# Column groups for a decay tree and for one layer's attention values, and four edits to VectorE's order, in a two-model transformer kernel

## The reference

```python
x = first_block(x, ...)          # layer 0 "even": gated convolution and pooling; layer 1 "odd"
return second_block(x, ...)      # layers 2 and 3, "hyb": hybrid_mixer

def odd_mixer(...):              # 8 heads: softmax(q k' + decay bias) v, and a 31-tap convolution
def hybrid_mixer(h, ...):
    a_out = rmsnorm(dilated_attention(rope(aq), rope(ak), av))
    o = gla_chunked(gq, gk, gv, log_sigmoid(z) / 16)    # gated linear attention, 4 heads
    g_out = rmsnorm(o) * silu(gr)
    return concatenate([a_out, g_out]) @ w_out

def gla_chunked(q, k, v, g):     # what it computes, without the chunks
    b = cumsum(g)
    attn[t, s] = sum_d q[t, d] k[s, d] exp(b[t, d] - b[s, d])    for s <= t
    return attn @ v
```

## Time and profile before

| | us |
|---|---|
| median of 3 runs | 1201.57 (1200.78 to 1203.65) |
| the profiled execution | 1202.72 |
| its span, first to last instruction | 1200.9 |
| PE busy | 1180.9 (98%) |
| PEld busy | 969.2 (81%) |
| DVE busy | 757.3 (63%) |
| ACT busy | 601.1 (50%) |
| granted clock of PE, mean | 0.999 |

### The profile page before, as it was taken

The page is one execution under the profiler, slowest core; times in us unless marked ns, Lnnn a source line. Parts: engine busy times, 40 slices in busy tenths (PEclk is TensorE's granted clock), DMA queues, the critical chain, the costliest instruction groups (busy, mean ns, idle before and its releaser), DMA issues.

```text
span 1200.9 us, 16977 instructions
## 1 busy us (share of the span) xinstructions
PE 1180.9 (98%) x5878; PEld 969.2 (81%) x5878; DVE 757.3 (63%) x1055; ACT 601.1 (50%) x896; POOL 44.5 (4%) x78
## 2 busy tenths in 40 slices
PE   8999999999999999999999999999999999999997
PEld 6877888888868888888778888888888878888886
DVE  4788545548887765554777676456366777755541
ACT  4555534425865554352555665445356566644530
POOL 0200000000001000000100100000010011000000
PEclk9999999999999999999999999999999999999999
DMA  7667765735633775662565157666626524856540
GB/s 255 186 226 223 250 205 179 232 116 164 206 122 107 226 243 179 209 220 96 164 203 177 50 166 257 195 195 208 192 84 223 167 72 133 266 180 209 165 150 35
DMA packets 161086, 214.14 MB, mean 178 GB/s; under 512 B 13137, under 2 KB 104953, under 8 KB 161024
## 3 DMA queue, kind: packets, MB, share of 16 engines
q1 hardware_dynamic: 155840, 201.52, 52.6%
q10 hardware_dynamic: 4896, 11.58, 2.9%
q0 software_dynamic: 288, 0.23, 0.2%
HBM read 212.22 MB, written 1.06 MB: 178 GB/s over the span
## 4 chain that ended last, share of the span: by engine, by line
PE 50%; DVE 0%; issue 0%; ACT 0%; POOL 0%; POOLq 0%; DVEq 0%; ACTq 0%
PE ps L577 15%; PE ps L579 15%; PE ps L578 15%; PE ps L920 2%; PE ps L1084 1%; PE ps L978 0%; PE ps L734 0%; PE ps L726 0%; PE ps L950 0%; PE ps L741 0%; PE ps L970 0%; PE ps L967 0%; PE ps L997 0%; PE ps L996 0%; PE ps L995 0%
## 5 line engine op out<-in xcount | busy, mean ns | idle before, releaser
L1540 DVE TENSOR_TENSOR w_lo<-raw,w_hi 128x1024 fp32r<-128x1024 f32 x377 | 446.9, 1222 | 132.6 <-ACT w_hi L1150 129.3
L1150 ACT ACTIVATE w_hi<-raw 128x1024 fp32r<-128x1024 f32 x377 | 381.2, 1054 | 137.4 <-PE ps L579 70.5
L577 PE MATMUL ps<-w_hi,a_hi 128*128 128x512 f32 x1040 | 414.2, 398 | 4.6 <-DVE w_lo L1540 1.6
L579 PE MATMUL ps<-w_hi,a_lo 128*128 128x512 f32 x1040 | 406.2, 391 | 0.0
L578 PE MATMUL ps<-w_lo,a_hi 128*128 128x512 f32 x1040 | 405.3, 390 | 0.0
L577 PEld LDWEIGHTS ps<-w_hi,a_hi 128*128 128x128 f32 x1040 | 195.6, 188 | 47.7 <-DVE a_lo L1558 3.4
L579 PEld LDWEIGHTS ps<-w_hi,a_lo 128*128 128x128 f32 x1040 | 195.5, 188 | 41.9
L578 PEld LDWEIGHTS ps<-w_lo,a_hi 128*128 128x128 f32 x1040 | 195.8, 188 | 37.9
L577 PE MATMUL ps<-w_hi,h_hi 128*128 128x512 f32 x480 | 188.6, 393 | 0.5 <-DVE h_lo L2002 0.4
L579 PE MATMUL ps<-w_hi,h_lo 128*128 128x512 f32 x480 | 187.0, 390 | 0.0
L578 PE MATMUL ps<-w_lo,h_hi 128*128 128x512 f32 x480 | 186.8, 389 | 0.0
(11 more groups left out here) (220 smaller groups left out, 763.6 us busy)
## 6 DMA issues: line engine op xcount, KB each, us to landing
raw<-ffn_w_in SPq DMA_DIRECT2D x176, 256.0 KB, 4.2
raw<-w_in SPq DMA_DIRECT2D x96, 256.0 KB, 3.2
raw<-ffn_w_out SPq DMA_DIRECT2D x88, 256.0 KB, 3.9
raw<-w_gate SPq DMA_DIRECT2D x88, 256.0 KB, 3.7
raw<-w_up SPq DMA_DIRECT2D x88, 256.0 KB, 4.4
raw<-w_down SPq DMA_DIRECT2D x88, 256.0 KB, 4.2
raw<-od_w_in SPq DMA_DIRECT2D x40, 256.0 KB, 3.0
raw<-ev_w_in SPq DMA_DIRECT2D x32, 256.0 KB, 4.3
```

The lines of the kernel that those rows point to most:

```text
L577: nc.tensor.matmul(ps[:, bank, :], hi, wh, start=first, stop=False)
L579: return nc.tensor.matmul(ps[:, bank, :], lo, wh, start=False, stop=last)
L1150: nc.scalar.activation(w_hi[:, v.slot, :], raw[:, v.raw, :], ACT.Copy).then_inc(w_high, 1)
L1540: V.tensor_tensor(w_lo[:, v.slot, :], raw[:, v.raw, :], w_hi[:, v.slot, :].bitcast(F32), ALU.subtract).then_inc(w_low, 1)
```

## The change

- `first_chunks`: at the first feed-forward boundary (kk = 1) PE turns tile 1 ahead of the third unit of the second chunk, not of the fourth.
- `after_boundary` and `boundary` on DVE: for k = 0 one unit fewer is fed ahead of tile 1's boundary; for k = 3 (the one boundary with a layer norm and a norm of the next model in one) a unit that was fed inside the boundary is fed ahead of it. For the others the order is the same.
- `level`: levels 0 and 4 to 8 take four matmuls instead of one, each for 32 tokens, on its own column group (32 or, in level 4, 16 stationary columns; 32 or 16 moving ones); level 3 takes two, level 2 one with 64 stationary columns instead of 128. Level 1 is as before.
- `keep` level 0: a predicated copy into `g_att`, which DVE now clears (`memset`, 128x1024) after the scans, instead of a product with the identity.
- `head_values`, `last_values`: in the odd layer four matmuls on four column groups (`in_groups`) instead of one; in the hybrid layers as before.
- `two_mixers` on PE: another order; the first tile's `turn_y` stands ahead of `last_values` and the second behind it.
- `two_mixers` on DVE: `head_lows` of heads 6 and 7 ahead of `linear_norm(0)`, `linear_norm(1)` behind the last `turned_weights`; `linear_norm` in four fused instructions instead of two.
- `odd_step`: the causal mask is added in step 3, ahead of `edges(1)` and of four units, instead of in step 4 behind them.

```diff
-                            if t == 0 and c == 1 and q == 3:
+                            if t == 0 and c == 1 and q == (2 if kk == 1 else 3):
                                 turn_x(kk, 1)
...
+                        at, m = kept_at(h, t) % 4, LEVELS[n - 1] if n else 0
+                        step = 2 * m if m >= 16 else 32
+                        for first in range(0, P, step):
+                            here = slice(P * t + first, P * t + first + step)
+                            if n == 0:
+                                ks, qs, rows_k, col, w = g_qkT[r, 2 + b, here], g_qkT[r, b, here], 32, P * at + first, 32
+                            else:
+                                ks = g_x[r, n % 2, b, here]
+                                qs, rows_k, col, w = right(ks, m), step, P // 2 * at + first // 2, step // 2
+                                if m >= 16:
+                                    ks, rows_k = g_x[r, n % 2, b, P * t + first:P * t + first + m], m
+                            mm = nc.tensor.matmul(tb[first:first + rows_k, h % 2, col:col + w], ks, qs, start=True, stop=True)
...
+            def in_groups(bank, turned, t, cols, first, last, narrow):
+                if not narrow:
+                    return nc.tensor.matmul(acc[:, bank, cols], turned, p_v[:, t, cols], start=first, stop=last)
+                for g in range(0, P, 32):
+                    mm = nc.tensor.matmul(acc[g:g + 32, bank, cols], turned[:, g:g + 32], p_v[:, t, cols], start=first, stop=last)
+                return mm
...
+                pair_logits(l, 2)
+                head_values(l, 0)
+                head_values(l, 1)
+                head_turn(l, 2)
+                head_turn(l, 3)
+                pair_logits(l, 3)
+                head_values(l, 2)
+                head_turn(l, 4)
+                head_values(l, 3)
+                head_turn(l, 5)
+                head_values(l, 4)
+                head_values(l, 5)
+                head_turn(l, 6)
+                head_turn(l, 7)
+                turn_y(l, g_normed, 0, (0,))
+                last_values(l)
+                turn_y(l, g_normed, 0, (1,))
...
-                if not (is_ln[k] and pre[k]):
-                    feed(end + 7)
-                boundary(k, 1, end + 7)
+                feed(end + (6 if k == 0 else 7))
+                boundary(k, 1)
                 feed(end + 8)
...
                 if c == 3:
                     convolve(2)
-                    feed(end)
-                    edges(1)
-                if c == 4:
                     dve.wait_ge(cum_spread, 16)
...
+                    edges(1)
+                    feed(end)
...
+                for h in range(GLA_H):
+                    cols = slice(GLA_DV * h, GLA_DV * (h + 1))
+                    ins = V.scalar_tensor_tensor(g_o[:, t, cols], acc[:, 1 + 2 * t, cols], g_rstd[:, t, h:h + 1], g_r[:, t, cols],
+                                                 ALU.mult, ALU.mult)
...
+            def two_mixers(l):
+                tile_done(dve, 1, l, "A", NA[l] - 1)
+                for j in range(HEADS // 2):
+                    head_lows(l, 2 * j)
+                    head_lows(l, 2 * j + 1)
+                    if j == 0:
+                        output_gate(l, 1)
+                    else:
+                        turned_weights(l, 2 * j - 1)
+                linear_norm(l, 0)
+                turned_weights(l, HEADS - 1)
+                linear_norm(l, 1)
+                split_y(l, (0, 1))
```

More of the change, by code:

```diff
@@ L912, in level @@
                         r, tok = level_rows(h)[0], slice(P * t, P * (t + 1))
-                        if n == 0:
-                            ks, qs, at, w = g_qkT[r, 2 + b, tok], g_qkT[r, b, tok], kept_at(h, t) % 4, P
-                        elif n == 1:
-                            ks, qs, at, w = g_x[r, 1, b, 0:P], g_x[r, 1, b, P:SEQ], far_at(h) % 2, P
-                        else:
-                            ks, at, w = g_x[r, n % 2, b, tok], kept_at(h, t) % 4, P // 2
-                            qs = right(ks, LEVELS[n - 1])
-                        mm = nc.tensor.matmul(tb[:, h % 2, w * at:w * (at + 1)], ks, qs, start=True, stop=True)
+                        if n == 1:
+                            at = far_at(h) % 2
+                            mm = nc.tensor.matmul(tb[:, h % 2, P * at:P * (at + 1)], g_x[r, 1, b, 0:P], g_x[r, 1, b, P:SEQ],
+                                                  start=True, stop=True)
+                            continue
+                        at, m = kept_at(h, t) % 4, LEVELS[n - 1] if n else 0
[10 more added lines that the diff above has]
+                            mm = nc.tensor.matmul(tb[first:first + rows_k, h % 2, col:col + w], ks, qs, start=True, stop=True)
                 mm.then_inc(g_pair.sem, 1)
@@ L984, in last_values @@
                     cols = slice(HD * h, HD * (h + 1))
-                    mm = nc.tensor.matmul(acc[:, 0, cols], probsT[:, h % 2, 0:P], p_v[:, 0, cols], start=True, stop=True)
+                    mm = in_groups(0, probsT[:, h % 2, 0:P], 0, cols, True, True, LAYERS[l] == "odd")
                 mm.then_inc(tile_attended.sem, 1)
@@ L993, in head_values @@
                 pT = probsT[:, h % 2, :]
+                narrow = LAYERS[l] == "odd"
                 if both:
-                    nc.tensor.matmul(acc[:, 0, cols], pT[:, 0:P], p_v[:, 0, cols], start=True, stop=True)
-                nc.tensor.matmul(acc[:, 2, cols], pT[:, P:2 * P], p_v[:, 0, cols], start=True, stop=False)
-                nc.tensor.matmul(acc[:, 2, cols], pT[:, 2 * P:3 * P], p_v[:, 1, cols], start=False,
-                                 stop=True).then_inc(attended.sem, 1)
+                    in_groups(0, pT[:, 0:P], 0, cols, True, True, narrow)
+                in_groups(2, pT[:, P:2 * P], 0, cols, True, False, narrow)
+                in_groups(2, pT[:, 2 * P:3 * P], 1, cols, False, True, narrow).then_inc(attended.sem, 1)
+            def in_groups(bank, turned, t, cols, first, last, narrow):
[4 more added lines that the diff above has]
+                return mm
             def turn_quads(bank, i):
@@ L1055, in two_mixers, with turn_y @@
                 head_turn(l, 1)
-                for j in range(HEADS // 2):
-                    if j + 2 < HEADS // 2:
-                        pair_logits(l, j + 2)
-                    if j == HEADS // 2 - 1:
-                        last_values(l)
-                        break
-                    for i in range(2):
-                        head_values(l, 2 * j + i)
-                        head_turn(l, 2 * j + 2 + i)
-                    if j == 2:
-                        turn_y(l, g_normed, 0)
-            def turn_y(l, ready, first):
+                pair_logits(l, 2)
[15 more added lines that the diff above has]
+                turn_y(l, g_normed, 0, (1,))
+            def turn_y(l, ready, first, tiles=range(NT)):
                 src = g_o if ready is g_normed else o_tok if LAYERS[l] == "odd" else y_tok
-                for t in range(NT):
+                for t in tiles:
                     pe.wait_ge(ready.sem, ready.at(l, t))
@@ L1566, in x_split, with boundary @@
                                     a_hi[:, part[0], part[1]].bitcast(F32), ALU.subtract).then_inc(x_low.sem, 1)
-            def boundary(k, t, units=0):
+            def boundary(k, t):
                 l, ffn = divmod(k, 2)
@@ L1629, in boundary @@
                     chain.step(V.tensor_tensor(nbuf[:, :], xt, pre_row(k), ALU.mult))
-                    feed(units)
                     chain.settle()
@@ L1859, in hyb_step @@
                     chain.settle()
+                if c == 1:
+                    chain.step(V.memset(g_att[:, :, :], 0.0))
+                    chain.settle()
                 for n in LEVELS_AFTER.get(c, ()):
@@ L1923, in linear_norm @@
                 dve.wait_ge(g_rooted.sem, g_rooted.at(l, 0))
-                chain.step(V.tensor_tensor(heads(g_o[:, t, :], GLA_H), heads(acc[:, 1 + 2 * t, :], GLA_H),
-                                           g_rstd[:, t, :].unsqueeze(2).broadcast_to([P, GLA_H, GLA_DV]), ALU.mult))
-                chain.settle()
-                V.tensor_tensor(g_o[:, t, :], g_o[:, t, :], g_r[:, t, :], ALU.mult).then_inc(g_normed.sem, 1)
-            def hyb_rest(l):
-                def beside(j):
-                    if j == 0:
-                        output_gate(l, 1)
-                    else:
-                        linear_norm(l, j - 2) if j > 1 else None
+                for h in range(GLA_H):
+                    cols = slice(GLA_DV * h, GLA_DV * (h + 1))
+                    ins = V.scalar_tensor_tensor(g_o[:, t, cols], acc[:, 1 + 2 * t, cols], g_rstd[:, t, h:h + 1], g_r[:, t, cols],
+                                                 ALU.mult, ALU.mult)
+                    if h < GLA_H - 1:
+                        chain.step(ins)
+                ins.then_inc(g_normed.sem, 1)
+            def hyb_rest(l):
                 output_gate(l, 0)
```

(2 more changed lines are left out.)

12 lines of the change are left out of this document (5 added, 7 removed).

## The result

The changed kernel takes **1194.65 us** (median of 5 runs, 1193.78 to 1196.04) against 1201.57 (the same median as above, now of 5 runs): the ratio is 0.9939, with a 95% interval of 0.9925 to 0.9954. 1192.3 was forecast, in a range of 1188.5 to 1199.0.

What follows compares the result with a forecast made beforehand. PE, busy 98% of the span, was taken as the bound: its issue intervals plus few waits. Terms -6.9 - 2.2 - 1.5 + 1.1 + 0.2 = -9.3 us, from 1201.57 to 1192.3 us, range 1188.5 to 1199.

Steps and rivals of the forecast that it cites:

- Decay tree: PE's tree levels in both hybrid layers: small passes on eight tiles start every 7 ns, 6.9 us less in all.
- rival 1: Tree: an issue cost shared by all groups; gain eaten at 19 ns a pass, 1210 us at 31 ns; chance 0.12.
- Rival 2: Tree: only four tiles at a time, or loads in a row; only levels 2 and 3 gain, 1197 us; chance 0.12.
- Clearing and predicated copy: DVE's work ahead of tree level 1: covered by two units of PE; uncovered, up to 1.7 us a layer.
- rival 4: DVE's moved work shows: clearing or mask not covered, about 2 us, 1194 to 1196 us; chance 0.06.
- Boundary k = 0: First feed-forward boundary: PE's turn starts at 93.6 and tile 1's units begin 1.5 us earlier.
- Odd layer: Odd layer's attention: earlier mask removes the second logits' wait (1.45), cheaper values add 0.75; 2.2 us less.
- The values in four groups: Odd layer's value matmuls on PE: 2.7 us less work, of which about 0.7 us comes through.
- Boundary k = 3: Unit moved from the wait for POOL, where it cost nothing, to ahead of tile 1's boundary: 1.1 us more.
- Two mixers: Hybrid layers' new order: the sixth head's turn gains, the shared values give it back; 0.1 us more a layer.
- Rival 3: Two mixers keep their gain if the splits overlap better: 1.4 us more a layer, 1189.5 us; chance 0.08.

Runs made afterwards that it cites:

- a_wide: The changed kernel with levels 0 and 4 to 8 of the decay tree on two column groups of 64 instead of four of 32: 1194.13 us, ratio 0.9919.
- a_bias: The changed kernel with the odd layer's bias transfer issued earlier on ACT's queue, two units behind the store of the sums: 1197.34 us, ratio 0.9957.
- a_order: The changed kernel with the clearing of the taps' edges and one weight unit ahead of the mask and its wait for the bias: 1192.46 us, ratio 0.9915.
- best: The changed kernel with a_order, a_fill, a_wide and the edit at k = 3 undone together: 1190.48 us, ratio 0.9897.
- a_fill: The changed kernel with four half-units instead of two ahead of the shared attention, and the second tile's turn a unit later: 1193.34 us, ratio 0.9913.

## Why the prediction was right, and where not

- **Decay tree, -6.9 forecast, -6.5 measured.** The step holds. The pace of small passes on eight tiles was taken as 7 ns; a level with 64 passes takes 0.55 us, 8.7 a pass, level 0 with twice the moving columns 0.56, 9.0 a pass, and level 3 with 32 passes on four tiles 0.26, 8.5 a pass. As neither 16 or 32 columns nor four or eight tiles change it by much, I read it as an issue pace that all groups share, rival 1 in kind but far below its break-even of 19 ns. (a_wide, with 64 columns a tile, came out as this reading said.) Of the 0.11 that it adds, 0.09 comes back in a shorter way out (0.11 instead of 0.20), and so 0.38 a level is left of 0.40. Only level 4 waits, 0.12, for DVE's factors. Rival 2 is out by the same starts. The Trainium skill's rule (TensorEngine Tiling, Instruction Overhead), an estimated 25 ns a pass, is contradicted by them too, even if its matmul is taken as two passes (17.4 ns).
- **Clearing and predicated copy, hidden.** PE has no wait between levels 0 and 1, so this half of rival 4 is out. The copy lasts 1.37 us for both halves.
- **Boundary k = 0, -1.5 forecast, -1.65 measured.** Every place came within 0.4 us. Over all kernels with this edit it is 1.3 to 1.7, and against the three old-order executions with a full clock there about 1.3 on the mean.
- **Odd layer, -2.2 forecast, -0.2 measured: the step that failed.** It is the sentence that the two additions "then move to 330.7 to 333.1", with the minima at 338.7. The minima did come at 338.79. But 330.7 is the landing of one transfer in one execution, and the sum takes off both this gain and k = 0's 1.5 us, as if the landing moved along: 3.7 together, where 1.9 came. The other half of rival 4, the mask's cover gone at about 2 us, is what happened, and its 1194 to 1196 holds the result. The 7.3 us of the earlier trace rows is the shortest of thirteen profiled executions (8.4 to 10.2 in the others). The transfer shares the DMA engines with the raw weights, which a_bias shows from the other side. I put the wait's cover right (what stands behind it has time) and then did not ask what the wait does to the next thing on the engine: edges and four units, 5.5 us, stood behind it, and with them the minima. In all six executions in which DVE stood for the bias the minima come 7.80 us behind its landing. a_order shows that the move is worth 2.4 more as soon as 2 us of this stand ahead of the wait. How much the odd layer as a whole gained depends on the execution it is held against: the six other than a_bias, a_order and `best` that have its new form average 0.2 below before's, and the four with the old form 0.5 above it. So it gained about 0.7, which is what the values bring; the mask's move brought nothing.
- **The values in four groups**: 0.7 of 2.7 us usable was forecast, 0.71 measured from the minima to the end of the attention: 20.58 or 20.59 in all nine executions with them, 21.28 or 21.29 in the four without.
- **Boundary k = 3, +1.1 forecast, +0.14 measured.** The unit is 1.14 earlier on the path, as said, but "where it cost nothing" was wrong: in POOL's wait it held POOL back by 0.98. The wait ahead of the turn is 0.83 and not 1.9, because the root came sooner.
- **Two mixers, +0.2 forecast, +0.12 measured**, with the wait for `y_tok` at 0.78 (0.8 forecast). Rival 3 is out. a_fill shows what the step lacked: work of PE for it to stand behind.
- The total: 9.3 us were forecast, 8.2 came between the profiled executions and 6.9 between the medians. That the 8.2 lies so near was partly luck: the misses of 2.0 us (odd layer) and 1.0 (k = 3) have opposite signs.

Open: why the low clock comes behind a wait in one execution and not in another, and why the transfer of the bias took 7.3 us in the one execution from which the forecast was made.

## What to carry to other kernels

When an instruction that waits for a transfer is moved ahead of ready work, the work moves behind the transfer: put what is ready ahead of the wait, and take the landing as a range, since a transfer's time depends on what else is under way. A gain upstream does not pass through a point that is tied to a transfer; check each saved microsecond against the next such point before adding terms. Split small matmuls over column groups as long as the array's tiles, and not the issue pace, are the limit; here two groups of 64 beat four of 32, by 0.05 us a level. Read a step from more than one execution before a few tenths are given a cause.

## What the runs showed of the hardware

- Matmuls of 64 rows by 16 or 32 stationary columns on four or eight tiles of the array start every 8.2 to 9.0 ns, counted in passes, over up to 64 in a row; with 64 columns on four tiles 14.5 to 15.4 ns (a_wide).
- A DVE instruction with two large inputs from the state buffer holds a POOL operation of 0.19 us until it ends (0.75, 1.17 and 1.28); beside one that reads from PSUM the operation keeps its 0.19.
- PE's clock fell to 1.2 GHz for some 3.4 us behind waits of 1.2 to 3.4 us in 6 of 13 profiled executions (the first 13 and the last 15 us aside), and behind similar ones it did not. In the changed kernel it fell behind the 1.65 us of line 977 and cost nothing: from the minima to the end of the attention it is 20.58 us there, and 20.59 in a_wide with a full clock.
- The same transfer of 1 MB took 7.3 to 10.2 us beside weight loads, and the 256 KB weight loads beside it took up to 7.9 us (a_fill), those just before it 2.5 to 4.0.
